# One weight remainder of every column set: by VectorE's subtraction, or by an adding DMA

## The chip, the core and the metric

The kernel runs on one core of a Trainium2 chip: TensorE (PE, with its weight loads shown apart as PEld), VectorE (DVE), ScalarE (ACT), GpSimd (POOL) and SyncE (SP), and 16 DMA engines that all queues share. The metric is the device time of one launch in microseconds (us).

## The reference, cut to what matters

```python
def swiglu(x, w_gate, w_up, w_down):
    return (jax.nn.silu(x @ w_gate) * (x @ w_up)) @ w_down
# trunk, for l in range(DEPTH):                       # DEPTH = 2, D = 1024, D_FF = 2816, all float32
    x = x + 0.5 * swiglu(rms_norm(x, g_norm[l, 0]), w_ffn_gate[l, 0], w_ffn_up[l, 0], w_ffn_down[l, 0])
    ...                                               # attention (two kinds), with its projections
    x = x + 0.5 * swiglu(rms_norm(x, g_norm[l, 2]), w_ffn_gate[l, 1], w_ffn_up[l, 1], w_ffn_down[l, 1])
```

The tokens are 512 of a prompt and 8 x 16 of running streams, 640 in all. The four SwiGLU blocks ("FFN 0" to "FFN 3") are where the change lies.

## The kernel before

**Two words for a number.** A float32 operand is used as two rounded words of the type fp32r: a high word (the value rounded) and a low word (value minus high word, the remainder). A product is three matmuls: high x high, high x low, low x high. For weights ACT makes the high word (an ACTIVATE Copy that rounds) and DVE the low word (`raw - high`, TENSOR_TENSOR subtract). In the attention's projections POOL does both.

**Sets and roles.** The 2816 FFN columns are taken 256 at a time, once for the gate and once for the up weight: one such 1024 x 256 block of weights is a "set". Groups of 2, 3, 3 and 3 such steps make 4, 6, 6 and 6 sets; after each group `ffn_down` (L885) multiplies the hidden rows by the down weight. FFN 0 handles its first two sets in another way, so there are 86 sets in 16 groups. Within a set the product is done by Winograd's 2 x 2 form of Strassen's scheme: a set's block is cut into four of 512 rows x 128 columns, W11 and W21 (upper rows, first and second columns), W12 and W22 (lower rows). A set needs seven products, with the weights W11, S1, S2, W12, S3, S4 (S1 to S4 are sums made by DVE, L2015) and W22. Each of the seven, a "role", has a place in SBUF of 1024 words a partition, 512 for the high and 512 for the low word (`role_at`, L298). W22 has one place of its own ("lo1", or "lo0" in groups that begin on an odd load), so that the W22 of a set can be written only when PE is done with the W22 of the set before.

**PE's order** (`products`, L78; `ffn_sets`, L827): for set s: W11(s), S4(s-1), S1(s), S2(s), W22(s-1), W12(s), S3(s). After a group's last set S4 and W22 follow at once. One product (L779) is 12 matmuls of 320 columns.

**ACT's order** (`ffn_sets`, L1548): W11(s+1), S4(s), S1(s+1), S2(s+1), W22(s), W12(s+1), S3(s+1), with copies between PSUM banks (L1523) and the hidden rows' Silu and rounding (L1539, L1546) between them. Each is a `role_high` (L1445) that waits for the data, and for PE to be done with the place.

**DVE's order** (`ffn_sets`, L2196): the sums (`role_sum`, L2015) and remainders (`role_low`, L2001) of the same roles, with the outputs of the products (L2153 to L2193) between them.

**Semaphores.** `w_cast` counts ACT's high words, `w_split` the finished remainders and `w_used` PE's finished products, all in the order of PE's products (a "unit" each). A load of SP waits on `w_split` until the raw words that it overwrites have been read (L486): the lower half of a set's raw words (`raw2`) comes free with that set's W22.

**SP** loads a set as two DMAs of 512 KB (L488), in two alternating pairs of buffers. **POOL** does nothing in the four FFNs; its code is a list of waits and splits for the projections and small copies in the attention.

```python
                if (f, g, s, role) in EARLY_COUNT:                                      # PE, L766
                    pe.wait_ge(sem("early_split"), EARLY_COUNT[f, g, s, role])
                else:
                    pe.wait_ge(w_split, UNIT[f, g, s, role] + 1)
```

Of the kernel before, what the change touches and what calls it, by code (L numbers as in the profile page):

```python
# [21 lines left out]
P = 128  # L22
# [65 lines left out]
class Plan:  # L88


    def __init__(self):
        self.unit, self.load, self.set, self.cast, self.sum = {}, {}, {}, {}, {}
        self.slot_free, self.raw_free, self.landed, self.landed2 = {}, {}, {}, {}
        self.units, self.loads, self.casts = 0, 0, 0
        self.slots, self.raws, self.slot, self.halves, self.landings = {}, {}, {}, [0, 0], [0, 0]
        self.ffn(0)
        self.tiles("qkv", QKV_TILES)
        self.tiles("oa", SQ_TILES, 1)
        self.ffn(1)
        self.tiles("kv", ROW_TILES)  # L100
        self.tiles("wf", 1)
        self.tiles("kv_rest", KV_TILES - ROW_TILES)
        self.ffn(2)
        self.tiles("qb", SQ_TILES)
        self.tiles("ob", SQ_TILES, 0)
        self.ffn(3)
# [36 lines left out]
    def ffn(self, f):  # L143
        for g, pairs in enumerate(GROUPS):
            sets, turned = sets_of(f, g), self.loads % 2
            for s in range(sets[0]):
                for role, slot in STANDARD[s]:
                    self.role((f, g, s, role), slot)
            for s, role in products(sets):
                slot = ROLE_SLOT[role]  # L150
                self.role((f, g, s, role), slot[:2] + str(1 - int(slot[2])) if turned and len(slot) == 3 else slot)
            for s in range(2 * pairs):
                key, early = (f, g, s), f in EARLY and (g, s) == (0, 0)
                p = self.next_load(key, not early)
                if not early:
                    self.halves[p] += 1
                    self.landed2[key] = 16 * self.halves[p]
                    for part, last in ((1, "S3" if s in sets else "W21"), (2, "W22")):
                        self.raw_free[key, part] = self.raws.get((p, part), -1) + 1
                        self.raws[p, part] = self.unit[f, g, s, last]  # L160
            for s in sets:
                self.set[f, g, s] = len(self.set)
            for s in range(sets[0] - 1, sets[-1] + 1):
                for key in ([(f, g, s, "S4")] if s in sets else []) + ([(f, g, s + 1, r) for r in SUMS[:3]] if s + 1 in sets else []):
                    self.sum[key] = len(self.sum) + 1
            self.tiles((f, g), KB, 0)
# [69 lines left out]
def yoco_stream_step(nc, x_prompt, x_sample, cache_a_k, cache_a_v, cache_b_k, cache_b_v, cache_b_logf,  # L236
# [4 lines left out]
    with ExitStack() as ctx:  # L241
# [406 lines left out]
        @block.gpsimd  # L648
        def _(pool):

            made = [0]

            def split(unit, slot, words, landed, made_by_now=None):
                pool.wait_ge(w_loaded[slot], landed)
                pool.wait_ge(w_used, unit - 1)
                pool.sem_inc(sem("pool_passed"), 1)
                pool.tensor_copy(w_hi[slot][:, 0:words], raw[slot][:, 0:words]).then_inc(w_hi_made, 1)  # L657
                pool.wait_ge(w_hi_made, made_by_now)
                pool.tensor_tensor(w_lo[slot][:, 0:words], raw[slot][:, 0:words],  # L659
                                   w_hi[slot][:, 0:words].bitcast(F32), ALU.subtract).then_inc(w_split, 1)  # L660

            def run(name, count):

                base, par, landed = BASE[name], SLOT[name], PLAN.landed
                pool.wait_ge(w_split, base)
                with pool.Fori(0, count // 2) as i:
                    for u in range(2):
                        split(base + i * 2 + u, (par + u) % 2, 1024, i * 16 + landed[name, u], made_by_now=i * 2 + (made[0] + u + 1))
                made[0] += count

            def stage(x, b):
                if b >= 1:
                    pool.wait_ge(sem("ss_ready" + x), b)
                at = slice(b * DS + NP, b * DS + NP + DS)
                qbd = queries[x]
                pool.tensor_copy(qbd[0:64, :, 0:DS], qh[0:64, :, at]).then_inc(sem("q_staged" + x), 1)
                pool.wait_ge(sem("q_staged" + x), 2 * b + 1)
                pool.tensor_copy(qbd[64:P, :, DS:2 * DS], qh[64:P, :, at]).then_inc(sem("q_staged" + x), 1)
                pool.wait_ge(sem("q_staged" + x), 2 * b + 2)

            def spread_rows(h):

                pool.wait_ge(sem(f"row_in{h % 2}"), h // 2 * 16 + 16)
                both = FP[:, h % 2].rearrange("p c k -> p (c k)")
                pool.partition_broadcast(both, both[0:1]).then_inc(sem("rows_spread"), 1)

            run("qkv", QKV_TILES)
            pool.wait_ge(sem("qbd_clearA"), 1)
            pool.wait_ge(sem("heads_read"), 20)
            for b in range(DB):  # L690
                stage("A", b)
            pool.wait_ge(w_split, BASE["oa"])
            split(BASE["oa"], SLOT["oa"], 1024, PLAN.landed["oa", 0], made_by_now=made[0] + 1)
            made[0] += 1
            run("kv", ROW_TILES)
            split(BASE["wf"], SLOT["wf"], 1024, PLAN.landed["wf", 0], made_by_now=made[0] + 1)
            made[0] += 1
            run("kv_rest", KV_TILES - ROW_TILES)
            run("qb", SQ_TILES)
            spread_rows(0)  # L700
            pool.wait_ge(sem("qbd_clearB"), 1)
            pool.wait_ge(sem("q_read"), PAIR)
            for b in range(DB):
                stage("B", b)
                if b + 1 < PAIR:
                    spread_rows(b + 1)


        @block.tensor
        def _(pe):  # L710
# [52 lines left out]
            def product(f, g, s, role, x, bank, start, marked=()):  # L763


                if (f, g, s, role) in EARLY_COUNT:  # L766
                    pe.wait_ge(sem("early_split"), EARLY_COUNT[f, g, s, role])
                else:
                    pe.wait_ge(w_split, UNIT[f, g, s, role] + 1)
                hi, lo = role_parts(f, g, s, role)  # L770
# [615 lines left out]
        def _(act):  # L1386
# [45 lines left out]
            def role_high(f, g, s, role):  # L1432
                key = (f, g, s, role)
                p, own = LOAD[f, g, s] % 2, set_at(f, g, s) is early
                if own:
                    act.wait_ge(sem("early_loaded"), 32 if f == 1 else 64)
                elif role in ("W11", "W21"):
                    act.wait_ge(w_loaded[p], PLAN.landed[f, g, s])
                elif role not in SUMS:
                    act.wait_ge(w_loaded2[p], PLAN.landed2[f, g, s])  # L1440
                if role in SUMS:
                    act.wait_ge(w_summed, PLAN.sum[key])
                if PLAN.slot_free[key]:
                    act.wait_ge(w_used, PLAN.slot_free[key])
                act.activation(role_parts(f, g, s, role)[0], role_source(f, g, s, role), ACT.Copy).then_inc(  # L1445
                    sem("early_cast") if key in EARLY_COUNT else w_cast, 1)

# [522 lines left out]
        def _(dve):  # L1970
# [15 lines left out]
                    dve.wait_ge(sem("sq_used"), event * KB + k)  # L1986
                    dve.tensor_tensor(sqacc[:, :], sqacc[:, :], t2[:, :], ALU.add).then_inc(sem("sq_used"), 1)

            def tile_low(name, m, words=1024):
                p = LOAD[name, m] % 2  # L1990
                dve.wait_ge(w_cast, PLAN.cast[name, m])
                dve.tensor_tensor(w_lo[p][:, 0:words], raw[p][:, 0:words], w_hi[p][:, 0:words].bitcast(F32), ALU.subtract).then_inc(w_split, 1)  # L1992

            def role_low(f, g, s, role):
                key = (f, g, s, role)
                hi, lo = role_parts(f, g, s, role)
                if key in EARLY_COUNT:
                    dve.wait_ge(sem("early_cast"), EARLY_COUNT[key])
                else:
                    dve.wait_ge(w_cast, PLAN.cast[key])  # L2000
                dve.tensor_tensor(lo, role_source(f, g, s, role), hi.bitcast(F32), ALU.subtract).then_inc(  # L2001
                    sem("early_split") if key in EARLY_COUNT else w_split, 1)

            def role_sum(f, g, s, role):
                p = LOAD[f, g, s] % 2
# [190 lines left out]
            def ffn_sets(f, g, root):  # L2196
                sets, n = sets_of(f, g), 2 * GROUPS[g]
                for s in sets:
# [14 lines left out]
                        role_low(f, g, s + 1, "S2")  # L2213
                    if more:
                        last_rows(f, g, s - 1)
                    role_low(f, g, s, "W22")
                    if not more and g == 0:
                        dve.wait_ge(sem("root_ready"), root)
                    first_rows(f, g, s)
                    if next_one:  # L2220
                        role_sum(f, g, s + 1, "S3")
                        role_low(f, g, s + 1, "W12")
                    if more and s % 2 == 0:
                        hidden_low(f, g, s - 1, 1)
                    if next_one:
                        role_low(f, g, s + 1, "S3")
                tile_low((f, g), 0, n * P)
                sums_out(f, g, n - 1)
                last_rows(f, g, n - 1)
                hidden_low(f, g, n - 1, 0)  # L2230
# [599 lines left out]
```

## Time and profile before

| | |
|---|---|
| median of 3 runs | 2512.87 us (2509.95 to 2515.33) |
| profiled execution, first to last instruction | 2512.1 us |
| PE busy | 2460.3 us (98%) |
| PE's weight loads busy | 2334.3 us (93%) |
| DVE busy | 1700.1 us (68%), 2964 instructions |
| ACT busy | 1135.3 us (45%) |
| POOL busy | 202.0 us (8%) |
| DMA traffic | 262.99 MB, 105 GB/s over the span |

The span of the profiled execution and the median of the runs agree within 0.8 us, so times read from the trace can be set against the median as they stand. "Busy" is the time in which an engine executes; a wait is listed with the engine, line and tile that ended it. In the timeline the columns are: start in us, duration in us, engine, line, instruction, output<-inputs by the program's areas, shape, and how many instructions were merged into the row (x12); in brackets the idle time ahead of it. Several roles can be merged into one row (x24 are two products). w_area and r_area hold the roles, R their raw words; k_area, v_area, x_area hold the activations.

### The profile page before, as it was taken

What the parts mean: (1) busy time and instruction counts of PE and PEld (TensorE: products, weight loads), DVE (VectorE), ACT (ScalarE), POOL (GpSimd) and SP (SyncE); (2) the same over time, 40 slices, a digit from 0 to 9 for tenths busy, and PEclk for the clock granted to TensorE, in tenths of its full rate; (3) what the DMA queues carried; (4) which work ended last, traced back from release to release, by engine and by line L of the source; (5) the groups of instructions that cost most, each with busy time, mean ns of one, the idle gap of its engine ahead of it and who ended that gap; (6) DMA issues with size and microseconds to landing.
All of it is one profiled execution on the core that took longest, in us unless ns stands there. A gap on an engine that the chain in (4) does not pass through costs nothing.

```text
span 2512.1 us, 46850 instructions
## 1 busy us (share of the span) xinstructions
PE 2460.3 (98%) x18869; PEld 2334.3 (93%) x18869; DVE 1700.1 (68%) x2964; ACT 1135.3 (45%) x2261; POOL 202.0 (8%) x144
## 2 busy tenths in 40 slices
PE   8999999899898999999999999999999999999998
PEld 8999999788678999999988999999996699999998
DVE  7777677322687877767734886758628887868585
ACT  6443444101785634344421643435418855535254
POOL 0000000454000000000045000000041000000000
PEclk9999999999999999999999999999999999999999
DMA  4323232232763232323223332323257631322222
GB/s 129 90 73 95 70 99 60 73 116 88 269 253 102 63 89 73 95 69 100 60 81 124 105 106 63 98 76 91 64 169 256 229 109 47 112 78 74 86 72 80
DMA packets 261489, 262.99 MB, mean 105 GB/s; under 512 B 13537, under 2 KB 222106, under 8 KB 261282
## 3 DMA queue, kind: packets, MB, share of 16 engines
q1 hardware_dynamic: 255536, 244.98, 31.1%
q10 hardware_dynamic: 5746, 15.12, 1.7%
q8 instruction: 146, 2.39, 0.4%
q14 instruction: 61, 0.50, 0.1%
HBM read 246.56 MB, written 13.51 MB: 104 GB/s over the span
## 4 chain that ended last, share of the span: by engine, by line
PE 90%; DVE 5%; ACT 3%; issue 2%; DMA 1%; POOL 0%; SPq 0%; DVEq 0%; ACTq 0%; POOLq 0%
PE PS L779 40%; PE PS L885 24%; PE PS L966 10%; PE PS L729 7%; PE PS L717 2%; PE PS L1167 1%; PE PS L712 1%; PE PS L1024 1%; PE PS L1125 1%; PE PS L1086 1%; DMA vreg<-in_cache_a_v_dram 1%; ACT R L1678 0%; ACT tt L1686 0%; DVE x_area L2060 0%; DVE tt L2370 0%
## 5 line engine op out<-in xcount | busy, mean ns | idle before, releaser
L779 PE MATMUL PS<-x_area,w_area 128*128 128x320 f32 x3096 | 482.1, 309 | 0.0
L779 PEld LDWEIGHTS PS<-x_area,w_area 128*128 128x128 f32 x3096 | 461.0, 188 | 0.2 <-DVE w_area L2001 0.2
L885 PE MATMUL PS<-r_area,w_area 128*128 128x320 f32 x2568 | 393.3, 309 | 0.0
L885 PEld LDWEIGHTS PS<-r_area,w_area 128*128 128x128 f32 x2568 | 380.6, 188 | 0.8 <-DVE r_area L2193 0.8
L1445 ACT ACTIVATE w_area<-R 128x512 fp32r<-128x512 f32 x341 | 213.0, 629 | 200.8 <-PE PS L779 133.6
L1992 DVE TENSOR_TENSOR w_area<-R,w_area 128x768 fp32r<-128x768 f32 (+2 forms) x143 | 132.4, 926 | 218.7 <-ACT w_area L1430 217.1
L2001 DVE TENSOR_TENSOR w_area<-R,w_area 128x512 fp32r<-128x512 f32 x341 | 234.3, 687 | 47.9 <-ACT w_area L1445 42.1
L966 PE MATMUL PS<-w_area,xn_hi 128*128 128x512 f32 x800 | 252.6, 397 | 6.6 <-POOL w_area L659 6.6
L1430 ACT ACTIVATE w_area<-R 128x768 fp32r<-128x768 f32 (+2 forms) x143 | 117.1, 819 | 308.2 <-PE PS L885 281.1
L885 PE MATMUL PS<-v_area,w_area 128*128 128x320 f32 x1620 | 253.4, 309 | 0.0
L885 PEld LDWEIGHTS PS<-v_area,w_area 128*128 128x128 f32 x1620 | 241.5, 188 | 0.3 <-DVE v_area L2193 0.3
L2015 DVE TENSOR_TENSOR R<-R 128x512 f32<-128x512 f32 x336 | 230.6, 686 | 3.5 <-DMA R<-in_w_ffn_gate_dram 0.9
L779 PE MATMUL PS<-k_area,r_area 128*128 128x320 f32 x1296 | 206.8, 309 | 0.0
L2001 DVE TENSOR_TENSOR r_area<-R,r_area 128x512 fp32r<-128x512 f32 x259 | 177.3, 690 | 41.0 <-ACT r_area L1445 38.2
L1445 ACT ACTIVATE r_area<-R 128x512 fp32r<-128x512 f32 x259 | 161.8, 625 | 87.0 <-DVE R L2015 78.4
L779 PEld LDWEIGHTS PS<-k_area,r_area 128*128 128x128 f32 x1296 | 194.3, 188 | 0.3
L657 POOL CAST w_area<-R 128x1024 fp32r<-128x1024 f32 x50 | 56.3, 1127 | 1557.3 <-PE PS L885 1397.4
L966 PEld LDWEIGHTS PS<-w_area,xn_hi 128*128 128x128 f32 x800 | 147.9, 189 | 35.7 <-POOL w_area L659 6.8
L1523 ACT ACTIVATE PS<-PS 128x320 f32<-128x320 f32 x258 | 106.7, 418 | 135.7 <-PE PS L779 135.2
L779 PE MATMUL PS<-x_area,r_area 128*128 128x320 f32 x1032 | 165.4, 309 | 0.5 <-issue 0.5
L966 PE MATMUL PS<-w_area,xn_lo 128*128 128x512 f32 x400 | 157.0, 392 | 0.0
L779 PEld LDWEIGHTS PS<-x_area,r_area 128*128 128x128 f32 x1032 | 154.8, 188 | 0.7 <-issue 0.7
(302 smaller groups left out, 3585.1 us busy)
## 6 DMA issues: line engine op xcount, KB each, us to landing
R<-in_w_ffn_up_dram SPq DMA_DIRECT2D x88, 512.0 KB, 3.8
R<-in_w_ffn_gate_dram SPq DMA_DIRECT2D x84, 512.0 KB, 3.8
R<-in_w_ffn_down_dram SPq DMA_DIRECT2D x96, 384.0 KB, 3.2
vreg<-in_cache_a_v_dram SPq DMA_DIRECT2D x8, 2048.0 KB, 9.1
vreg<-in_cache_b_v_dram SPq DMA_DIRECT2D x8, 2048.0 KB, 8.8
R<-in_cache_a_k_dram SPq DMA_DIRECT2D x14, 1024.0 KB, 7.4
R<-in_cache_b_k_dram SPq DMA_DIRECT2D x14, 1024.0 KB, 8.8
R<-in_w_qkv_a_dram SPq DMA_DIRECT2D x24, 512.0 KB, 3.7
```

Source lines behind the costliest of these rows:

```text
L657: pool.tensor_copy(w_hi[slot][:, 0:words], raw[slot][:, 0:words]).then_inc(w_hi_made, 1)
L717: return pe.transpose(dst, src[rows], cst[rows, IDENT + 64 * r:IDENT + 64 * r + 64])
L729: last = pe.matmul(out[:, h, :], a[slot][:, w], x[:, k, h * HT:(h + 1) * HT], start=(k == 0 and a is w_hi and x is x_hi), stop=(k == kb - ...
L779: last = pe.matmul(PS[:, bank, 0:HT], a[:, k, :], b[:, k, :], start=(start and k == 0 and a is hi and b is x_hi), stop=(k == 3 and a is lo ...
L885: last = pe.matmul(out[:, h, :], a[slot][:, w], x[:, h * HT:(h + 1) * HT], start=(k == 0 and a is w_hi and x is hi), stop=(k == n - 1 and ...
L966: last = pe.matmul(PS[:, t, :], x[:, k, cols], a[s][:, w], start=(k == 0 and x is xn_hi and a is w_hi), stop=(k == KB - 1 and x is xn_lo))
L1430: act.activation(w_hi[p][:, 0:words], raw[p][:, 0:words], ACT.Copy).then_inc(w_cast, 1)
L1445: act.activation(role_parts(f, g, s, role)[0], role_source(f, g, s, role), ACT.Copy).then_inc(sem("early_cast") if key in EARLY_COUNT else ...
L1523: act.activation(PS[:, to, 0:HT], PS[:, of, 0:HT], ACT.Copy).then_inc(sem("copied"), 1)
L1992: dve.tensor_tensor(w_lo[p][:, 0:words], raw[p][:, 0:words], w_hi[p][:, 0:words].bitcast(F32), ALU.subtract).then_inc(w_split, 1)
L2001: dve.tensor_tensor(lo, role_source(f, g, s, role), hi.bitcast(F32), ALU.subtract).then_inc(sem("early_split") if key in EARLY_COUNT else ...
L2015: dve.tensor_tensor(*at, ALU.add).then_inc(w_summed, 1)
```

## The change

ACT writes two words for the role W22: as before the high word, and then, into the place of the low word, the rounded weight with its sign turned (an ACTIVATE Copy with scale -1.0). Then POOL issues a DMA that reads W22's 512 x 128 weights once more from HBM and adds them to what is there (`accum_op=ALU.add`), so that the place holds weight minus high word. PE waits on a new semaphore, `low_added`, for the W22 products. DVE's subtraction for W22 goes. What counted `w_split` for it is now counted with the next remainder: the W12 of the next set, or the first down tile after a group's last set, adds 2 in place of 1. The wait of SP for the lower raw half of a set (`raw2`) stands as it was, and so is met by that later count.

```diff
+            def last_lows(f):
+                for g in range(len(GROUPS)):
+                    for s in sets_of(f, g):
+                        w = (w_ffn_gate, w_ffn_up)[s % 2][f // 2, f % 2]
+                        at = (sum(GROUPS[:g]) + s // 2) * 2 * P + P
+                        pool.wait_ge(w_cast, PLAN.cast[f, g, s, "W22"])
+                        pool.dma_start(role_parts(f, g, s, "W22")[1], w[512:1024, at:at + P].rearrange("(k p) m -> p k m", p=P),
+                                       accum_op=ALU.add).then_inc(sem("low_added"), 16)
...                                         # called on POOL ahead of, between and after its other work, once for each FFN
@@ PE, product
+                elif role == "W22":
+                    pe.wait_ge(sem("low_added"), 16 * PLAN.added[f, g, s])
@@ ACT, role_high
+                if role == "W22" and (f, g, s) in PLAN.added:
+                    act.activation(role_parts(f, g, s, role)[0], role_source(f, g, s, role), ACT.Copy)
+                    act.activation(role_parts(f, g, s, role)[1], role_source(f, g, s, role), ACT.Copy, scale=-1.0).then_inc(w_cast, 1)
+                    return
@@ DVE, ffn_sets
-                    role_low(f, g, s, "W22")
...
-                        role_low(f, g, s + 1, "W12")
+                        role_low(f, g, s + 1, "W12", 2)
...
-                tile_low((f, g), 0, n * P)
+                tile_low((f, g), 0, n * P, 2)
```

On DVE, in the first set of FFN 0's second group, these instructions stood (in this order: the remainder of S4, two sums, the remainders of S1 and S2, that of W22, the first output rows L2153, the sum S3, and the remainders of W12 and S3):

```order
L2001 TENSOR_TENSOR w_area<-R,w_area 128x512 [waits w_cast]
L2015 TENSOR_TENSOR R<-R 128x512 [waits w2_loaded1,w_loaded1]
L2015 TENSOR_TENSOR R<-R 128x512 [waits w_summed]
L2001 TENSOR_TENSOR r_area<-R,r_area 128x512 [waits w_cast] x2
L2001 TENSOR_TENSOR w_area<-R,w_area 128x512 [waits w_cast]
L2153 TENSOR_TENSOR tt<-PS,rB 128x320 [waits w_used]
L2015 TENSOR_TENSOR R<-R 128x4x128
L2001 TENSOR_TENSOR w_area<-R,w_area 128x512 [waits w_cast] x2
```

and now (the lines have moved: 2022 is the remainder, 2036 the sum, 2174 the first rows):

```order
L2022 TENSOR_TENSOR w_area<-R,w_area 128x512 [waits w_cast]
L2036 TENSOR_TENSOR R<-R 128x512 [waits w2_loaded1,w_loaded1]
L2036 TENSOR_TENSOR R<-R 128x512 [waits w_summed]
L2022 TENSOR_TENSOR r_area<-R,r_area 128x512 [waits w_cast] x2
L2174 TENSOR_TENSOR tt<-PS,rB 128x320 [waits w_used]
L2036 TENSOR_TENSOR R<-R 128x4x128
L2022 TENSOR_TENSOR w_area<-R,w_area 128x512 [waits w_cast] x2
```

The row of W22 between the remainders of S1, S2 and the first output rows is gone; nothing else moved.

On ACT, in the same set, stood the copy of the fifth block, the high words of S4, of S1 and S2, of W22, of W12, and a copy in PSUM:

```order
L1531 ACTIVATE R<-PS 128x320 [waits sum_read,w_used]
L1445 ACTIVATE w_area<-R 128x512 [waits w_used,w_summed]
L1445 ACTIVATE r_area<-R 128x512 [waits w_used,w_summed] x2
L1445 ACTIVATE w_area<-R 128x512 [waits w_used,w2_loaded0]
L1445 ACTIVATE w_area<-R 128x512 [waits w_used,w2_loaded1]
L1523 ACTIVATE PS<-PS 128x320 [waits last_rows_read,w_used]
```

and now (1463 and 1464 are W22's two words):

```order
L1552 ACTIVATE R<-PS 128x320 [waits sum_read,w_used]
L1466 ACTIVATE w_area<-R 128x512 [waits w_used,w_summed]
L1466 ACTIVATE r_area<-R 128x512 [waits w_used,w_summed] x2
L1463 ACTIVATE w_area<-R 128x512 [waits w_used,w2_loaded0]
L1464 ACTIVATE w_area<-R 128x512
L1466 ACTIVATE w_area<-R 128x512 [waits w_used,w2_loaded1]
L1544 ACTIVATE PS<-PS 128x320 [waits last_rows_read,w_used]
```

One instruction came in, between W22's high word and that of W12. On POOL, the first of the 86 DMAs, ahead of its first loop:

```order
L695 DMA w_area<-in_w_ffn_gate_dram 128x4x128 [waits w_cast]
L695 DMA w_area<-in_w_ffn_up_dram 128x4x128 [waits w_cast]
L695 DMA w_area<-in_w_ffn_gate_dram 128x4x128 [waits w_cast]
L695 DMA w_area<-in_w_ffn_up_dram 128x4x128 [waits w_cast]
L695 DMA w_area<-in_w_ffn_gate_dram 128x4x128 [waits w_cast]
```

Each writes 128 partitions, in four pieces of 128 words (512 bytes) each: 256 KB.

## Rows read from the trace of the kernel before

**Rows 1.** The page: busy time, share of the span, instructions of each engine.

```profile
PE 2460.3 (98%) x18869; PEld 2334.3 (93%) x18869; DVE 1700.1 (68%) x2964; ACT 1135.3 (45%) x2261; POOL 202.0 (8%) x144
```

**Rows 2.** Waits of PE, whole span: waiter <- releaser: us, times, longest.

```profile
PE PS L966 <- POOL w_area L659: 6.6, 1, 6.6
...
PE PS L779 <- ACT PS L1523: 1.8, 3, 1.0
...
PE PS L779 <- DVE r_area L2001: 1.7, 1, 1.7
PE PS L789 <- DVE r_area L2001: 1.4, 1, 1.4
```

**Rows 3.** Busy by stretch: FFN 0's last group (six sets): length, each engine, clock, DMA.

```profile
335.40:409.40 74.00, 74.00 (x507) 74.00 (x506) 56.93 (x95) 38.68 (x72) 0.00 (x0) 1.00 0.23 68
```

**Rows 4.** One line's instructions: duration min/median/max ns, first and last start, forms.

```profile
L2001 DVE TENSOR_TENSOR w_area<-R,w_area x341: 679/686/694, 17.6 to 2447.3; 128x512 fp32r<-128x512 f32 x171
...
L1445 ACT ACTIVATE w_area<-R x341: 613/633/637, 16.6 to 2446.6; 128x512 fp32r<-128x512 f32 x171
```

**Rows 5.** Timeline: a group's first set, W22's high word (first of two), later its product.

```profile
344.97 1.14 ACT L1445 ACTIVATE w_area<-R 128x512 fp32r<-128x512 f32 x2
...
351.28 3.56 PEld L779 LDWEIGHTS PS<-x_area,w_area 128*128 128x128 f32 x24
```

**Rows 6.** Timeline: the second set, and the third, the same two.

```profile
354.22 0.62 ACT L1445 ACTIVATE w_area<-R 128x512 fp32r<-128x512 f32 x1
...
363.60 3.56 PEld L779 LDWEIGHTS PS<-x_area,w_area 128*128 128x128 f32 x24
...
365.76 0.64 ACT L1445 ACTIVATE w_area<-R 128x512 fp32r<-128x512 f32 x1 [0.47 <-PE PS L779]
...
375.92 3.56 PEld L779 LDWEIGHTS PS<-x_area,w_area 128*128 128x128 f32 x24
```

**Rows 7.** Timeline: the last set; the x24 are S4 and W22.

```profile
402.72 0.63 ACT L1445 ACTIVATE w_area<-R 128x512 fp32r<-128x512 f32 x1 [1.05 <-PE PS L779]
...
405.84 3.56 PEld L779 LDWEIGHTS PS<-x_area,w_area 128*128 128x128 f32 x24
```

**Rows 8.** Timeline: the first set of FFN 1, W22's high word and product.

```profile
853.60 0.62 ACT L1445 ACTIVATE w_area<-vN 128x512 fp32r<-128x512 f32 x1
...
857.26 3.56 PEld L779 LDWEIGHTS PS<-x_area,w_area 128*128 128x128 f32 x24
```

**Rows 9.** Timeline: W22 and W12's remainders, the set's loads, the next sums from them.

```profile
345.70 0.69 DVE L2001 TENSOR_TENSOR w_area<-R,w_area 128x512 fp32r<-128x512 f32 x1
...
347.31 1.48 DVE L2001 TENSOR_TENSOR w_area<-R,w_area 128x512 fp32r<-128x512 f32 x2
...
335.53 11.26 SPq L488 DMA_DIRECT2D R<-in_w_ffn_gate_dram  x2
...
352.24 1.41 DVE L2015 TENSOR_TENSOR R<-R 128x512 f32<-128x512 f32 x2
...
360.08 1.80 PEld L779 LDWEIGHTS PS<-k_area,r_area 128*128 128x128 f32 x12
```

**Rows 10.** DMA issues of the page: KB each, median us to landing.

```profile
R<-in_w_ffn_up_dram SPq DMA_DIRECT2D x88, 512.0 KB, 3.8
...
R<-in_w_ffn_down_dram SPq DMA_DIRECT2D x32, 256.0 KB, 2.7
...
out_dram<-vN ACTq DMA_DIRECT2D x2, 512.0 KB, 12.2
```

**Rows 11.** POOL's instructions on their lines.

```profile
L659 POOL TENSOR_TENSOR w_area<-R,w_area x50: 2355/2399/3508, 455.6 to 1867.3; 128x1024 fp32r<-128x1024 f32 x50
```

More of the change, by code:

```diff
@@ L91, in __init__ @@
     def __init__(self):
-        self.unit, self.load, self.set, self.cast, self.sum = {}, {}, {}, {}, {}
+        self.unit, self.load, self.set, self.cast, self.sum, self.added = {}, {}, {}, {}, {}, {}
         self.slot_free, self.raw_free, self.landed, self.landed2 = {}, {}, {}, {}
@@ L162, in ffn @@
                 self.set[f, g, s] = len(self.set)
+                self.added[f, g, s] = len(self.added) + 1
             for s in range(sets[0] - 1, sets[-1] + 1):
@@ L685, in spread_rows @@
                 pool.partition_broadcast(both, both[0:1]).then_inc(sem("rows_spread"), 1)
+            def last_lows(f):
[6 more added lines that the diff above has]
+                                       accum_op=ALU.add).then_inc(sem("low_added"), 16)
+            last_lows(0)
             run("qkv", QKV_TILES)
@@ L694, in _ @@
             made[0] += 1
+            last_lows(1)
             run("kv", ROW_TILES)
@@ L698, in _ @@
             run("kv_rest", KV_TILES - ROW_TILES)
+            last_lows(2)
             run("qb", SQ_TILES)
@@ L706, in _ @@
                     spread_rows(b + 1)
+            last_lows(3)
         @block.tensor
@@ L1987, in add_square, with tile_low, role_low @@
                     dve.tensor_tensor(sqacc[:, :], sqacc[:, :], t2[:, :], ALU.add).then_inc(sem("sq_used"), 1)
-            def tile_low(name, m, words=1024):
+            def tile_low(name, m, words=1024, units=1):
                 p = LOAD[name, m] % 2
                 dve.wait_ge(w_cast, PLAN.cast[name, m])
-                dve.tensor_tensor(w_lo[p][:, 0:words], raw[p][:, 0:words], w_hi[p][:, 0:words].bitcast(F32), ALU.subtract).then_inc(w_split, 1)
-            def role_low(f, g, s, role):
+                dve.tensor_tensor(w_lo[p][:, 0:words], raw[p][:, 0:words], w_hi[p][:, 0:words].bitcast(F32), ALU.subtract).then_inc(w_split, units)
+            def role_low(f, g, s, role, units=1):
                 key = (f, g, s, role)
@@ L2001, in role_low @@
                 dve.tensor_tensor(lo, role_source(f, g, s, role), hi.bitcast(F32), ALU.subtract).then_inc(
-                    sem("early_split") if key in EARLY_COUNT else w_split, 1)
+                    sem("early_split") if key in EARLY_COUNT else w_split, units)
             def role_sum(f, g, s, role):
```

## The prediction

> **What bounds the kernel now.** I read the busy times first: PE is busy 98% of the span, DVE 68%, ACT 45%, POOL 8% [rows 1]. The change takes work from DVE, so the next view is what PE waits for. Over the whole span the longest entries are single waits in the attention's projections; what the FFN products (L779, L789) wait for DVE's remainders is 1.7 + 1.4 us [rows 2]. In the stretch of FFN 0's last group (74.00 us, six sets) PE is busy 74.00 us at full clock while DVE does 56.93 and ACT 38.68 [rows 3]. DVE is therefore not late anywhere in the FFNs, and work taken from it can return the 3.1 us of these waits at most. The reader is to see that the gain is bounded by a PE that has no gap. A loss is not bounded: in a stretch without a gap each us by which a weight comes late is a us of the run. The question of the change is how early W22 is now, and what stands in the place of that lead.
>
> **The lead of W22 today.** Timeline of the four kinds of set, from the end of ACT's high word to PE's first weight load of the product:
> - first set of a group: the x2 are W22 and W12, so W22 ends at 344.97 + 0.63 = 345.60; the product begins at 351.28 [rows 5]: 5.7 us
> - second set: 354.84 to 363.60, 8.8 us; the following ones, 366.40 to 375.92, 9.5 us [rows 6]
> - last set: 403.35 to 405.84 + 1.76 (S4's half of the 3.56 us) = 407.60 [rows 7]: 4.25 us.
> There are 16 first, 16 last, 15 second and 39 middle sets among the 86 (the group of two sets in FFN 0 has a first and a last). The lead can't grow: ACT's instruction in the middle sets is released by PE's W22 of the set before (the 0.47 us wait in rows 6), because the place is the same, and the next W22 product stands seven products or 375.92 - 363.60 = 12.32 us later.
>
> **The change, part by part.**
> 1. *DVE's subtraction goes:* 86 x 0.687 us (median 686, [rows 4]) = 59 us less busy time on DVE. Returned to the run: between 0 and 3.1 us; I take 0, since they are two single waits, neither of them on w_area.
> 2. *ACT's second word:* 86 x 0.625 us (613 to 637, [rows 4]) = 54 us more on ACT, busy 1189. It delays the W12 word behind it by 0.6 us. In the first set that one ends at 346.11 [rows 5] and its remainder is done by 348.0 [rows 9], while its product stands behind W22's at 353.04: 5 us of cover, cost 0. It also takes 0.6 us from W22's own lead. What is left for the DMA: 5.1 us (first), 8.2 (second), 8.9 (middle), 3.7 (last).
> 3. *The DMA.* Let L be the time from ACT's second word to PE's seeing `low_added`. The run pays 16 (L - 3.7) + 16 (L - 5.1) + 15 (L - 8.2) + 39 (L - 8.9), each bracket where it is positive. No instruction of the trace adds by DMA, or has POOL issue one, so L is bounded. From below: SP's load of the same shape (256 KB, 512-byte pieces) lands 2.7 us after issue [rows 10]; then nothing is paid but in three or four opening sets (point 4). From above: the longest landing of 512 KB, 12.2 us [rows 10]; then 16 x 8.5 + 16 x 7.1 + 15 x 4.0 + 39 x 3.3 = 438 us. Between: the adding DMA reads 256 KB from HBM and 256 KB from its destination, as much as a 512 KB load, which lands after 3.8 us [rows 10]. Ahead of it POOL must work out 512 pieces in software, for source and destination; the nearest row is POOL's own instruction with two inputs, 2.4 us (2.5 in a longer one) [rows 11]. With 0.2 us of semaphores L = 3.8 + 2.5 + 0.2 = 6.5 us, an estimate. That makes 16 x 2.8 = 45 us in the last sets. In the first sets the DMA runs while SP's load of the next lower half (issued at about 346.4, and after the change at 347.3, [rows 9]) is on the same engines; for this I add 0.7 us, half of a load's transport: 16 x (7.2 - 5.1) = 34 us. In second and middle sets it is hidden.
> 4. *FFNs' opening sets:* in the first set of FFN 1 the lead is 857.26 - 854.22 = 3.0 us [rows 8], 2.7 less than in the other groups. For four FFNs at 2 us each: 8 us.
> 5. *The wait moves to another count.* `w_split` for W22 now comes with W12's remainder, at about 347.3 (347.31 + 0.69, less the 0.69 that DVE no longer spends ahead of it) in place of 346.4 [rows 9]. SP, which stands at that wait with all later loads behind it, issues the lower half 0.9 us later in the first set (some 2 us in others). It lands 3.7 us after, at 351.0; DVE's sums S1 and S2 start at 352.24, and their first product is at 360.08 [rows 9]. That is 1.2 us to the sum and another 6 to PE: cost 0. If the cover were gone, it would be DVE that idles first, and PE only past 6 us.
> 6. *POOL* waits in order in its queue: behind the waiting DMA stand the next FFN DMA, or the projections' splits. The splits are later work in any case, since they wait for that FFN's down tiles. Cost 0. Traffic rises by 86 x 256 KB = 22.5 MB to 285 MB at 23% of the DMA engines in this stretch [rows 3]: room enough.
>
> Sum: 0 + 0 + 45 + 34 + 8 + 0 = 87 us on 2512.1; the median of the runs is 0.8 us above that span, so 2600 us, 3.5% slower. What the step is: VectorE's 0.69 us, which had 4 to 9 us of slack, is replaced by a chain of 7 us.
>
> **Rivals.**
> *The DMA is hidden (not slower).* Place: the last sets, with 3.7 us, decide. If L is at most 3.7 us, only openings pay, under 5 us. For it: the 2.7 us of the same shape from SP; the spare DMA engines. Against: that row has neither software in front nor a read of the destination. Time 2513 to 2518. The Trainium skill ("DMA: Bandwidth & Descriptors", Anatomy of one DMA) has a fit for DMAs issued from GpSimd, 2.0 us plus the bytes at 436 GB/s; it would give 2.6 us here and so this rival. No run here shows that fit, and it was not made for 512-byte pieces or for adding. I give the rival 0.13.
>
> *The chain becomes the period of every set.* From L = 8.9 us on, W22's place can't be turned round within 12.32 us: product 1.76, ACT's two words 1.2 with 0.5 of release, and L. Then all 86 sets pay. At L = 11: 16 x 7.3 + 16 x 6.6 + 15 x 2.8 + 39 x 2.1 + 8 = 354 us, 2867 us. For it: landings of 12.2 us for 512 KB exist, and software that makes 1024 entries one by one could take far more than POOL's vector instruction. Against: only stores land that late. Chance 0.22.
>
> *DVE's relief shows (faster).* At most 3.1 us in rows 2 and what DVE gives the last groups: 2508 at best, and only together with a hidden DMA. Chance 0.02. That the change doesn't do what it says is excluded by the order: 86 remainders are gone from DVE, 86 words came on ACT and 86 DMAs on POOL.
>
> **How the numbers follow.** Forecast (L from about 4 to 8.9 us) 0.63, hidden 0.13, period 0.22, faster 0.02. Within the forecast the time goes from 2520 (L = 4) to 2512.9 + 16 x 5.2 + 16 x 4.5 + 15 x 0.7 + 8 = 2687 (L = 8.9, with 0.7 for the collision in the first sets); this is its own range. The whole range takes in the nearer half of the period rival: at L = 9.8 16 x 6.1 + 16 x 5.4 + 15 x 1.6 + 39 x 0.9 + 8 = 251, so up to 2765; below it stops at 2519 and leaves out most of the hidden case. What a measurement here can tell from no change is 0.2%, 5 us: slower 0.86, within it 0.12, faster 0.02.
>
> **What would show the steps.** In the changed profile PE's waits at the product line should be for the DMA on w_area, in 32 groups of about 2 to 3 us, at the end of each group and in its first set, and none in the middle. DVE's busy time should be about 1641 us and ACT's 1189. The stretch of one six-set group should be 74 + 5 us. If waits stand in every set, L is over 8.9 and the period rival holds; if PE's busy share in the group stays at 100%, the DMA is hidden. The time from the end of ACT's second word to the landing is L itself. Wrong would be a wait at products other than W22's (then the loads of point 5 are late), or a lower granted clock after the new gaps, which now is 1.00 in this stretch [rows 3].

## The result, and the profile after

| | before | after |
|---|---|---|
| median of the runs | 2511.91 us (2509.95 to 2515.33, 4 runs) | 2563.77 us (2559.39 to 2565.53, 4 runs) |
| ratio | | 1.0198, interval 1.0186 to 1.0210 |
| span of the profiled execution | 2512.1 us | 2563.7 us |

The change makes the kernel 2.0% slower, 52 us. The forecast was 87 us (2600 us, range 2519 to 2765). Direction and place came out as forecast, and the size is 0.6 of it.

The busy times of the page after, against [rows 1]:

```profile
PE 2471.7 (96%) x18869; PEld 2338.9 (91%) x18869; DVE 1652.1 (64%) x2878; ACT 1177.3 (46%) x2347; POOL 312.0 (12%) x230
```

DVE lost its 86 instructions and 48 us, ACT has 86 more and 42 us more, POOL 86 more and 110 us more (1.28 us for each DMA that it issues). PE issues the same 18869 matmuls, and its share fell from 98% to 96%: it now waits. For what, the waits of PE over the whole span say (waiter, releaser: us, times, longest; L796 is the line of the FFN products, L779 and L789 before), against [rows 2]:

```profile
PE PS L796 <- DMA w_area<-in_w_ffn_up_dram: 15.8, 16, 1.2
PE PS L796 <- DMA w_area<-in_w_ffn_gate_dram: 15.5, 11, 1.8
PE PS L983 <- POOL w_area L660: 6.6, 1, 6.6
PE PS L796 <- issue: 6.3, 4, 2.3
PE PS L796 <- ACT PS L1544: 5.1, 3, 3.1
PE PS L796 <- DVE r_area L2022: 1.8, 2, 1.7
```

The two DMA rows are new: 31.3 us in 27 waits for the adding DMA. The other five of the 32 waits at W22 stand in two rows that existed before: three of the four "issue" waits (5.8 us, all in first sets that open an FFN), and two of ACT's three (4.2 us). L1544 is the copy of an open accumulation in PSUM (L1523 in [rows 2]); in these two places it stands beside the same late word, and the profile names the later of the two. The remaining wait of each row, under 1 us, was there before, and so was the 6.6 us of the projection. The same 507 matmuls of FFN 0's last group, against [rows 3] (length, each engine, clock, DMA share):

```profile
343.60:420.65 77.05, 74.45 (x507) 73.98 (x506) 54.05 (x89) 41.94 (x79) 7.72 (x6) 1.00 0.39 90
```

The six sets take 77.05 us in place of 74.00, at full clock, with PE idle for 2.6 us of them where it had no gap. The prediction said 79 us.

How the first set of this group runs, in its timeline (start, busy us, engine, line; in brackets the wait and its releaser), against [rows 5] and [rows 9]:

```profile
353.12 0.62 ACT L1463 ACTIVATE w_area<-R 128x512 fp32r<-128x512 f32 x1
353.64 0.62 ACT L1464 ACTIVATE w_area<-R 128x512 fp32r<-128x512 f32 x1
354.55 1.28 POOL L695 DMA_DIRECT2D w_area<-in_w_ffn_gate_dram  x1 [58.29 <-ACT w_area L1464]
355.60 0.37 SPq L489 DMA_DIRECT2D R<-in_w_ffn_gate_dram  x1
356.72 0.37 SPq L489 DMA_DIRECT2D R<-in_w_ffn_up_dram  x1
357.67 1.80 PEld L796 LDWEIGHTS PS<-x_area,r_area 128*128 128x128 f32 x12
361.30 0.96 PE L796 MATMUL PS<-x_area,w_area 128*128 128x320 f32 x5 [1.56 <-DMA w_area<-in_w_ffn_gate_dram]
361.57 0.69 DVE L2036 TENSOR_TENSOR R<-R 128x512 f32<-128x512 f32 x1 [1.34 <-DMA R<-in_w_ffn_gate_dram]
```

ACT's negated word ends at 354.26. POOL starts 0.29 us later and is busy for 1.28 us. SP's load of the next lower half goes out at 355.60, while the adding DMA is under way. PE ends the product ahead and stands until 361.30. DVE too is late here, by the load that now comes later.

The last set, against [rows 7]:

```profile
414.12 1.28 POOL L695 DMA_DIRECT2D w_area<-in_w_ffn_up_dram  x1 [11.04 <-ACT w_area L1464]
415.79 1.80 PEld L796 LDWEIGHTS PS<-x_area,w_area 128*128 128x128 f32 x12
418.86 1.76 PEld L796 LDWEIGHTS PS<-x_area,w_area 128*128 128x128 f32 x12 [1.27 <-issue]
418.89 2.00 PE L796 MATMUL PS<-x_area,w_area 128*128 128x320 f32 x12 [1.04 <-DMA w_area<-in_w_ffn_up_dram]
```

Before, S4 and W22 were one unbroken row of 24 weight loads (3.56 us). Now it falls in two, with 1.27 us between them. In the third set nothing breaks:

```profile
377.15 1.29 POOL L695 DMA_DIRECT2D w_area<-in_w_ffn_gate_dram  x1 [10.63 <-ACT w_area L1464]
...
385.87 3.56 PEld L796 LDWEIGHTS PS<-x_area,w_area 128*128 128x128 f32 x24
```

From 377.15 to 385.87 there are 8.7 us, and the DMA needs 4.7. The adding DMA by itself: POOL's instruction (min/median/max ns), then the time from issue to landing, and SP's row of the page's DMA issues (count, KB each, median us):

```profile
L695 POOL DMA_DIRECT2D w_area<-in_w_ffn_gate_dram x43: 1273/1282/1473, 63.0 to 2486.1; - x43
...
DMA to landing us min/median/max: 4.3/4.7/6.6
```

```profile
R<-in_w_ffn_up_dram SPq DMA_DIRECT2D x88, 512.0 KB, 4.9
```

SP's own 512 KB load went from 3.8 us [rows 10] to 4.9. The first sets alone don't make that: in the experiments below the median is 4.9 us with the inner sets alone by DMA, 4.0 us with the edge sets alone, and 5.0 us with the load held out of the first sets' way. Whether the adding DMAs on the same engines or SP's later and closer issues do it was not separated.

I read L, from the end of ACT's negated word to the landing, and the stall of PE at W22, set by set. The stall is the idle time of PE's weight loads ahead of W22's product, and what its twelve loads then took beyond the 1.76 us of full clock:

| sets | L us, median (range) | stall us, all | each |
|---|---|---|---|
| 16 last | 4.88 (4.65 to 5.08) | 19.5 | 1.22 |
| 16 first | 6.62 (5.00 to 7.16) | 32.7 | median 1.68 |
| 15 second, 39 middle | 4.92 and 4.99 (4.56 to 6.56) | 0 | 0 |

The sum is 52.2 us, and the spans differ by 51.6. In PE's own account that is 40.3 us more idle time and 11.4 us more busy time. The whole loss lies in 32 of the 86 sets.

### The profile page after: what moved, and what is told of

Same layout as the page of the kernel before. It is cut to its first block, busy times and chain, and to the rows that moved or that the text cites. A ratio compares the mean times of both kernels' runs of the same rounds, so it can differ in the third digit from the quotient of the medians.

```text
span 2563.7 us, 47022 instructions
## 1 busy us (share of the span) xinstructions
PE 2471.7 (96%) x18869; PEld 2338.9 (91%) x18869; DVE 1652.1 (64%) x2878; ACT 1177.3 (46%) x2347; POOL 312.0 (12%) x230
## 4 chain that ended last, share of the span: by engine, by line
PE 83%; DMA 6%; DVE 4%; ACT 4%; issue 3%; POOL 0%; ACTq 0%; SPq 0%; DVEq 0%; POOLq 0%
PE PS L796 33%; PE PS L902 24%; PE PS L983 10%; PE PS L744 7%; DMA w_area<-in_w_ffn_up_dram 3%; DMA w_area<-in_w_ffn_gate_dram 3%; PE PS L732 2%; PE PS L1184 1%; PE PS L1041 1%; PE PS L727 1%; PE PS L1142 1%; ACT w_area L1464 1%; ACT w_area L1463 1%; PE PS L1103 1%; PE PS L1114 1%
## 5 line engine op out<-in xcount | busy, mean ns | idle before, releaser
L796 PE MATMUL PS<-x_area,w_area 128*128 128x320 f32 x3096 | 492.6, 312 | 41.2 <-DMA w_area<-in_w_ffn_up_dram 15.8
L796 PEld LDWEIGHTS PS<-x_area,w_area 128*128 128x128 f32 x3096 | 466.0, 190 | 48.9 <-issue 26.0
L1466 ACT ACTIVATE w_area<-R 128x512 fp32r<-128x512 f32 x257 | 161.3, 629 | 163.3 <-PE PS L796 113.1
L2022 DVE TENSOR_TENSOR w_area<-R,w_area 128x512 fp32r<-128x512 f32 x257 | 176.6, 688 | 58.0 <-ACT w_area L1466 54.4
L796 PE MATMUL PS<-k_area,r_area 128*128 128x320 f32 x1296 | 206.8, 309 | 0.0
L695 POOL DMA_DIRECT2D w_area<-in_w_ffn_gate_dram x43 | 55.7, 1295 | 1237.0 <-ACT w_area L1464 1078.2
L796 PEld LDWEIGHTS PS<-k_area,r_area 128*128 128x128 f32 x1296 | 194.3, 188 | 0.3
L1544 ACT ACTIVATE PS<-PS 128x320 f32<-128x320 f32 x258 | 106.9, 418 | 131.8 <-PE PS L796 131.3
L796 PE MATMUL PS<-x_area,r_area 128*128 128x320 f32 x1032 | 165.6, 309 | 0.8 <-issue 0.5
L796 PEld LDWEIGHTS PS<-x_area,r_area 128*128 128x128 f32 x1032 | 154.8, 188 | 1.5 <-ACT PS L1544 0.8
```

The costliest lines, as they stand in the source:

```text
L695: pool.dma_start(role_parts(f, g, s, "W22")[1], w[512:1024, at:at + P].rearrange("(k p) m -> p k m", p=P), accum_op=ALU.add).then_inc(sem( ...
L796: last = pe.matmul(PS[:, bank, 0:HT], a[:, k, :], b[:, k, :], start=(start and k == 0 and a is hi and b is x_hi), stop=(k == 3 and a is lo ...
L1544: act.activation(PS[:, to, 0:HT], PS[:, of, 0:HT], ACT.Copy).then_inc(sem("copied"), 1)
```

## The experiments

**Where the loss is: only the inner sets, or only the edge sets, by DMA.** Two complements. `by_dma` also selects POOL's list, PE's wait and DVE's subtraction for the other sets.

```diff
+def by_dma(f, g, s):
+    first, last = sets_of(f, g)[0], sets_of(f, g)[-1]
+    return first < s < last          # e1_inner
+    return s in (first, last)        # e2_edges
...
+                    if not by_dma(f, g, s):
+                        role_low(f, g, s, "W22")
```

> Theory (only a group's first and last sets pay; the 54 others have 8.2 to 8.9 us of lead against 4.9 that the DMA takes): the 54 inner sets' W22 by adding DMA, the 32 edge sets' by DVE as before. The time is that of the kernel before within 0.2% (2512 us), with no wait for the DMA at the product line. Rival (each adding DMA costs something wherever it stands, through the DMA engines that it shares or through the later count of w_split): 54/86 of the 52 us, about 2545 us.

> Theory: the 32 edge sets alone by adding DMA cost all of it, 2564 us within 3 us. Rival (each of the 86 costs the same 0.6 us): 32 x 0.6 = 19 us, about 2531 us.

Measured: the inner 54 sets by DMA, 2515.58 us, ratio 1.0008 (0.9999 to 1.0017, 11 runs against 21). The edge 32 sets by DMA, 2562.98 us, ratio 1.0201 (1.0185 to 1.0216). The busy row and the six-set stretch of the inner version, then the waits of PE in the edge version:

```profile
PE 2461.6 (98%) x18869; PEld 2335.0 (93%) x18869; DVE 1668.3 (66%) x2910; ACT 1156.7 (46%) x2315; POOL 271.3 (11%) x198
...
335.40:409.40 74.00, 74.00 (x507) 74.00 (x506) 54.69 (x90) 40.37 (x76) 5.13 (x4) 1.00 0.34 83
```

```profile
PE PS L803 <- DMA w_area<-in_w_ffn_up_dram: 16.6, 16, 1.5
PE PS L803 <- DMA w_area<-in_w_ffn_gate_dram: 14.1, 10, 1.6
PE PS L803 <- ACT PS L1551: 6.9, 5, 3.4
```

With the four inner DMAs PE is again busy for 74.00 of 74.00 us. The edges alone make the whole loss. This also settles three costs that I had put at nothing: 54 DMAs, 54 later `w_split` counts and 14 MB more traffic together move the time by 0.08%, and by 0.17% at the end of the interval. And DVE, with 32 us less to do, gives PE nothing.

**ACT's word alone.** The kernel before with the second word on ACT, and DVE's subtraction left to write over it.

```diff
+                if role == "W22" and (f, g, s) in PLAN.set:
+                    act.activation(role_parts(f, g, s, role)[0], role_source(f, g, s, role), ACT.Copy)
+                    act.activation(role_parts(f, g, s, role)[1], role_source(f, g, s, role), ACT.Copy, scale=-1.0).then_inc(w_cast, 1)
```

> The kernel before with ACT's second word in all 86 sets, and DVE's subtraction written over it as before (no DMA). Theory (the word is hidden): 2512 us within 0.2%, ACT 54 us busier. Rival (the word delays W12 and the copies behind it on ACT, and PE's waits come in part from there): 5 to 20 us slower, with waits of PE for ACT's copies at L1523.

Measured: 2513.87 us, ratio 1.0002 (0.9993 to 1.0011).

```profile
PE 2461.5 (98%) x18869; PEld 2334.9 (93%) x18869; DVE 1698.4 (68%) x2964; ACT 1174.2 (47%) x2347; POOL 201.2 (8%) x144
```

ACT's busy time rises by 39 us, and not by 54, in part since a word that waits for nothing starts 0.52 us after the one ahead and overlaps it by 0.1, and busy time counts an overlap once. Cost 0, as in part 2.

**The collision in the first sets.** SP's load is held until the adding DMA of the first set has landed.

```diff
+                    if part == 1 and s - 2 == sets_of(f, g)[0]:
+                        sp.wait_ge(sem("low_added"), 16 * PLAN.added[f, g, s - 2])
```

> The changed kernel, in which SP's load of the lower half that comes free with a first set's W22 is held until the adding DMA of that set has landed. Theory (the first sets' DMA takes 6.6 us in place of 4.9 because it runs beside this 512 KB load): it lands after 4.9 us in first sets too, and their stall falls from 1.7 to about 0.1 us: 2564 - 27 = 2537 us, unless the later load makes DVE's sums late for PE. Rival (the longer time comes from what DVE, ACT and POOL do there, not from the load): the landing stays at 6.6 us and the time at 2564 us or more.

Measured: 2549.51 us, ratio 1.0146 (1.0130 to 1.0162). The first set of the same group:

```profile
352.17 0.62 ACT L1466 ACTIVATE w_area<-R 128x512 fp32r<-128x512 f32 x1
...
353.08 1.28 POOL L697 DMA_DIRECT2D w_area<-in_w_ffn_gate_dram  x1 [58.23 <-ACT w_area L1466]
357.61 0.37 SPq L491 DMA_DIRECT2D R<-in_w_ffn_gate_dram  x1
357.96 3.56 PEld L798 LDWEIGHTS PS<-x_area,w_area 128*128 128x128 f32 x24
```

The load waits until 357.61, and the 24 weight loads are whole again. Over the 16 first sets L falls from 6.62 to 4.92 us, the value of all others, and the stalls from 32.7 to 8.7 us, all of that in the four openings. So 1.7 us of L in a first set was the collision. The time came down by only 14 us where 24 were taken away: PE now waits 8.1 us at S3's product of the third set, in 11 groups (0.74 each), for words made from the held load, and 1.8 us at W22 of three second sets, whose negated word stands on ACT behind the high words of S1 and S2 from that load. My 2537 us named the load's own deadline and gave it no price.

**What L is made of.** Three versions of POOL's DMA, the rest unchanged: without the addition; with the same bytes in 128 pieces of 2 KB; with half the rows, 256 pieces of 512 bytes.

```diff
+                        pool.dma_start(role_parts(f, g, s, "W22")[1], w[512:1024, at:at + P]...)        # e5_plain
+                        pool.dma_start(flat, w[512:640, min(at, 2304):min(at, 2304) + 512], accum_op=ALU.add)  # e6_rows
+                        pool.dma_start(role_parts(f, g, s, "W22")[1][:, 0:2], w[512:768, at:at + P]..., accum_op=ALU.add)  # e7_half
```

> The changed kernel with POOL's 86 DMAs plain copies in place of adding ones (the low word of W22 is then the weight itself: the addition is left out). The changed kernel's DMA lands 4.9 us after ACT's second word, of which 0.3 are ahead of POOL's instruction and 1.28 its duration; SP's plain load of the same shape lands in 2.7. Theory (reading the destination and adding it costs about 1 us): the landing falls to 3.9 us, the last sets' stall from 1.2 to 0.2, the time to about 2535 us. Rival (what costs is POOL's software, the addition is free): the landing stays at 4.8 to 4.9 us, the time at 2560 to 2564 us.

> The changed kernel with the same 256 KB added by each DMA, but read as 128 rows of 512 words that lie together: 128 pieces of 2 KB in place of 512 of 512 bytes (other weights are then added than the right ones). Theory (POOL works out piece by piece, and so do the DMA engines): POOL's instruction falls from 1.28 to 0.4 to 0.7 us, the landing from 4.9 to about 3.7 us, the time to 2530 us or less. Rival (a DMA of POOL has a fixed cost): POOL's 1.28 us and the landing of 4.9 us stay.

> The changed kernel with only the first two of the four 128-row parts added (256 pieces, 128 KB; the other half of the low word stays the negated weight). Theory (cost by piece): half of what depends on pieces and bytes goes, the landing falls from 4.9 to about 4.2 us, POOL's instruction to 0.7 to 0.9 us, the last sets' stall to 0.5, the time to about 2540 us. Rival (fixed cost): 4.7 us or more, and 2558 us or more.

One execution each, in which the kernel before took 2512.66 us (the median of 7). POOL's instruction and the landing, plain:

```profile
L695 POOL DMA_DIRECT2D w_area<-in_w_ffn_gate_dram x43: 742/742/942, 63.2 to 2437.4; - x43
...
DMA to landing us min/median/max: 3.2/3.3/5.0
```

in 2 KB pieces, adding:

```profile
L696 POOL DMA_DIRECT2D w_area<-in_w_ffn_gate_dram x43: 853/862/1063, 63.0 to 2451.8; - x43
...
DMA to landing us min/median/max: 4.0/4.3/5.3
```

and half the rows, adding:

```profile
L695 POOL DMA_DIRECT2D w_area<-in_w_ffn_gate_dram x43: 1194/1203/1377, 63.6 to 2441.1; - x43
...
DMA to landing us min/median/max: 3.3/3.6/5.2
```

| version | pieces, KB | POOL us | L, last sets | L, first sets | stalls, last + first | time |
|---|---|---|---|---|---|---|
| after | 512, 256 | 1.28 | 4.88 | 6.62 | 19.5 + 32.7 | 2563.77 |
| 2 KB pieces | 128, 256 | 0.86 | 4.52 | 4.53 | 13.7 + 7.2 | 2531.22 |
| half the rows | 256, 128 | 1.20 | 3.79 | 4.09 | 2.6 + 3.9 | 2517.5 |
| no addition | 512, 256 | 0.74 | 3.62 | 3.74 | 0.3 + 3.0 | 2515.77 |

The addition costs 4.88 - 3.62 = 1.26 us of L, of which 0.54 are in POOL's instruction. The rest is in the transport. The two pages have the packets of POOL's queue, and the time that they took as a share of 16 engines' span, the changed kernel first, then the plain one:

```profile
q0 software_dynamic: 45408, 22.55, 7.2%
...
q0 software_dynamic: 45408, 22.55, 4.8%
```

That is 65 ns a packet against 42, and at 33 packets for each engine and DMA it makes 0.7 us. The addition decides the loss: the plain DMA has L just under the 3.7 us of the last sets, and its kernel is 3 us from the one before. The pieces come next: the same bytes in a quarter of the pieces land 0.4 us earlier in last sets, which is what POOL's instruction is shorter by (1.28 to 0.86), and the first sets pay only in the openings.

In the two columns of L, SP's load holds up the addition in 512 pieces by far the most (4.88 to 6.62); half the rows lose 0.3 us, the plain DMA (3.62 to 3.74) and the addition in 128 pieces (4.52 to 4.53) hardly anything. This doesn't show that the kind of DMA makes the collision, since the overlap differs too. By the packets of the 12 first sets that open no FFN (medians), SP's first packet comes 2.5 us after POOL's issue in the changed kernel, 0.5 us after the first packet of the adding DMA: 87% of its packets start after that, and 540 KB of SP's two loads start before it is through. In the other three versions 31 to 39% of the packets start after SP's first, and 100 to 160 KB of SP's loads come between. In the middle sets of the changed kernel, where the share is 17%, L is 4.99 us. So the bytes that come between are a rival that these runs leave standing; it was not separated further.

The Trainium skill ("DMA: Bandwidth & Descriptors", Anatomy of one DMA) has 2.0 us plus the bytes at 436 GB/s for a DMA issued from GpSimd, an estimate of 2.6 us here. The plain DMA took 3.3 us to land and the adding one 4.7; the measurement decides. In the prediction I wrote that the fit was not made for 512-byte pieces or for adding; the page names neither a size of pieces nor adding for it, so it says less than that.

**The law of the leads, pushed past 8.9 us.** Four copies on POOL of the negated word onto itself, ahead of each DMA, planned as 2.4 us.

```diff
+                        for n in range(4):
+                            pool.tensor_copy(low, low.bitcast(F32)).then_inc(x_in[0], 1)
+                            pool.wait_ge(x_in[0], 32 + 4 * PLAN.added[f, g, s] - 3 + n)
```

> The changed kernel with four copies of the low word onto itself on POOL ahead of each DMA, some 0.6 us each, so that each DMA starts 2.4 us later (and POOL is busy in between). Theory (each set pays what is over its lead): last sets 1.2 + 2.4 = 3.6 us, first sets 1.7 + 2.4 or a little less (the collision with SP's load gets smaller) = 3.5 to 4.1, all others nothing, since 4.9 + 2.4 = 7.3 is under 8.2: 2564 + 32 x 2.1 to 32 x 2.4 = 2631 to 2641 us, and more by the clock: where a stall is over 3 us the granted clock falls to half for 3.4 to 6.8 us (it did so in three first sets), at 1.5 to 2.5 us each up to 32 x 2.5 = 80 us more, 2710 us. Rival (the half clock in three places had to do with the opening sets, not with the length of the stall): no more than 2645 us and no new stretches at half clock.

Measured: 2780.81 us (2772.87 to 2791.71), ratio 1.1063 (1.1028 to 1.1099), far past my figure. The copies, and the waits of PE:

```profile
L697 POOL CAST w_area<-w_area x344: 607/617/1137, 62.9 to 2713.4; 128x512 fp32r<-128x512 f32 x172
```

```profile
PE PS L800 <- DMA w_area<-in_w_ffn_up_dram: 94.4, 38, 5.0
PE PS L800 <- DMA w_area<-in_w_ffn_gate_dram: 64.9, 28, 4.6
PE PS L800 <- issue: 25.3, 5, 6.3
```

The copies took 0.61 to 1.14 us (mean 0.78), and four of them delayed the DMA by 4.2 us in first sets, 3.4 in middle and 2.7 in last ones, not by 2.4. The timeline shows beside what; a middle set, then the last set, with four copies each:

```profile
945.16 3.33 POOL L697 CAST w_area<-w_area 128x512 fp32r<-128x512 f32 x4 [7.59 <-ACT w_area L1468]
...
946.92 1.09 DVE L2026 TENSOR_TENSOR w_area<-R,w_area 128x512 fp32r<-128x512 f32 x1
...
949.08 0.68 DVE L2026 TENSOR_TENSOR w_area<-R,w_area 128x512 fp32r<-128x512 f32 x1
...
959.21 2.65 POOL L697 CAST w_area<-w_area 128x512 fp32r<-128x512 f32 x4 [9.16 <-ACT w_area L1468]
```

Beside the copies DVE's remainder took 1.09 us, right behind them 0.68; and where DVE waits for PE, the four copies took 2.65 us and not 3.33. The Trainium skill ("SBUF — State Buffer", Who interferes with whom) says that a VectorE instruction with two SBUF inputs contends with a GpSimd instruction that reads SBUF. The trace agrees, 1.09 against 0.68 us. With medians of L = 9.6 (first), 10.9 (second), 10.0 (middle) and 7.7 (last) every kind of set pays, as the rival of the period said of L over 8.9: 103.3, 26.7, 38.8 and 84.0 us (all first and last sets, 11 of the 15 second and 34 of the 39 middle ones). By the leads alone, 16 x 4.5 + 15 x 2.7 + 39 x 1.1 + 16 x 4.0 = 220 us. The stalls read are 253, which hold W22's products at a lower clock, and the span is 269 over that of before. Behind a stall at a last set:

```profile
962.16 1.27 POOL L699 DMA_DIRECT2D w_area<-in_w_ffn_up_dram  x1 [0.30 <-POOL w_area L697]
968.16 3.17 PEld L800 LDWEIGHTS PS<-x_area,w_area 128*128 128x128 f32 x12 [5.24 <-issue]
```

and two stretches of this kernel, columns as in [rows 3]:

```profile
965.70:972.50 6.80, 4.31 (x16) 4.34 (x17) 0.74 (x2) 0.31 (x2) 0.00 (x0) 0.50 0.33 57
...
940.00:965.00 25.00, 21.68 (x147) 21.18 (x145) 15.10 (x24) 11.22 (x21) 8.14 (x10) 1.00 0.21 31
```

Twelve weight loads took 3.17 us against 1.76 us, at a granted clock of 0.50, the 1.2 GHz level. There are 44 such stretches with 186 us at that level; before it was 7 with 31 us. So the rival that the clock stays as it was (2645 us at most) falls. PE was busy for 160 us of those 186, and before for 24 of the 31. At half the clock half of the difference is lost, (160 - 24) / 2 = 68 us, an estimate; the other 201 us of the 269 are waits, where the leads say 220. The clock's price thus came out within the 80 us that I allowed; what I had too small was the delay of the DMA, and with it L in second and middle sets. The limit of 3 us in that expectation isn't one that the rows show. In the three first sets that it points at, PE's weight loads had been idle for 2.06, 3.30 and 2.56 us, and in another for 2.12 us with the clock at 1.00 after it.

## Why the prediction was right in direction and too large

**The bound, and point 1 (DVE).** Right. PE had no gap, and DVE's 48 us returned nothing; the inner version has 32 us of the same relief and no gain. I had put 59 us: the durations of DVE's instructions do fall by 60 us in all, but neighbours overlap, and busy time counts an overlap once. The same holds for ACT, 42 us for 54.

**Point 2 (ACT).** Right: cost 0 by the run with the word alone.

**The leads.** Predicted 3.7, 5.1 and 8.9 us; measured 3.66 (last), 4.94 (first), 9.0 (middle). The mechanism, a lead against L in each kind of set, needed no change. One sum of the prediction is off: at L = 4 the formula with its openings gives 2526 us, not 2520.

**Point 3 (L) is the step that was mis-sized.** I put L = 3.8 + 2.5 + 0.2 = 6.5 us; the last sets have 4.88:

| part of L | predicted | measured |
|---|---|---|
| semaphore to POOL | 0.2 | 0.29 |
| POOL's instruction | 2.5 | 1.28 |
| from its end to the landing | 3.8 | 3.3 |
| collision, first sets only | 0.7 | 1.7 |

I took POOL's part from the row of its two-input tensor instruction [rows 11], which does other work of another length. It was the nearest row only because that engine had no other. For the last sets the term was 45 us and came to 19.5. For the first sets it was 34 and came to 27.5, because two errors met: L too large by 1.6, the collision too small by 1.0. That collision was the sum's one term for contention, and the run with the held load showed it by taking it away: L fell to 4.92 us against a lead of 4.94, and the stalls of the first sets by 24 us. Outside the openings, then, a first set pays for the collision alone.

**Point 4 (openings).** 8 us predicted. The four first sets that open an FFN stalled for 1.79, 2.11, 4.84 and 3.19 us (in the last two W22's product ran slowly; ahead of it the weight loads were idle for 3.30 and 2.56); over the other first sets that is 5.2 us more. With 27.5 and 19.5 that is the 52 us.

**Point 5 (later loads).** Cost 0, and nearly so, but with less to spare than I wrote. I counted 1.2 us to the sums. DVE waited 16.0 us for those loads in 17 waits, where it had waited 0.9, because the load also lands later (4.9 and not 3.8 us):

```profile
  DVE R L2036: 16.0, 17
```

PE's 6 us behind it covered this: PE's waits for DVE's remainders are 1.8 us in two waits, where they were 3.1 [rows 2].

**The clock, which I named and did not price.** The profile was to show by it that I was wrong. The mean is 0.991, and three stretches behind stalls in first sets are new; two of them, columns as in [rows 3], and the timeline where one begins:

```profile
1434.40:1441.30 6.90, 5.71 (x21) 5.74 (x22) 3.73 (x6) 4.39 (x8) 0.63 (x1) 0.51 0.33 108
...
2127.30:2130.70 3.40, 3.40 (x15) 3.40 (x14) 2.42 (x4) 3.08 (x6) 0.27 (x1) 0.51 0.01 4
```

```profile
1435.56 6.08 PEld L796 LDWEIGHTS PS<-x_area,w_area 128*128 128x128 f32 x24 [3.30 <-ACT PS L1544]
```

PE stood for 3.30 us, and 24 weight loads then took 6.08 us and not 3.56. In all, 45.9 us ran at the 1.2 GHz level against 30.9 before, with PE busy for 34.5 and 23.7 of them. Its price, half of that difference and so some 5 us (an estimate), is inside the 32.7 us of the first sets. It is a small part of the 52, and the first sets' number is not L alone.

**The rivals.** Hidden: it needs L up to 3.7 us, and the plain DMA of the experiment shows that case, 3 us from no change. The rival's own price for the transport (2.7 us, SP's row) was too low by 0.6 plain and 2.0 adding. Period: false at L = 4.9, borne out for most inner sets at L = 10. No version here beats the kernel before: with a PE without gaps the best that a hidden DMA can do is the inner version's ratio of 1.0008.

## What to carry to other kernels

When the busiest engine has no gap, taking work from another returns nothing, so price a replacement by latency alone: measure the lead of each instance, at the edges of a loop too, and set the new chain's length against it. Here 54 of 86 instances were free and 32 cost 52 us. Where no row shows an operation, a row of another operation on the same engine bounds nothing; ask also which transfer starts at the same moment, since that one was the largest term here: 24 us of stalls, against 19.5 in the last sets.

## What the runs showed of the hardware

- An adding DMA of 256 KB in 512 pieces, issued by POOL, held POOL for 1.28 us and landed 4.7 us after its issue; the same without the addition 0.74 and 3.3 us; adding in 128 pieces 0.86 and 4.3 us.
- The addition took 65 ns a packet in place of 42, in pieces of 512 bytes.
- Beside SP's loads of 512 KB it landed as late as 6.6 us after its issue; with the load held back, the same DMAs had L = 4.92 in place of 6.62 us. Without the addition or in 128 pieces the delay was 0.12 us or less, but with far less of SP's loads in between. The loads' median went from 3.8 to 4.9 us.
- Stalls of PE of 2 to 5 us were followed in some places by 3.4 to 6.9 us at a granted clock of 0.5, in others by none (2.06 and 2.12 us of idle weight loads, the one with it and the other without). What tells the two apart was not tried.
- POOL's 128x512 copy took 0.61 us alone and up to 1.14 us beside DVE's work, and DVE's 128x512 remainder 1.09 us beside it against 0.68.
